# Expert weights in 2 MB transfers, gate and up by column halves, and a spare slot used once

## The reference, cut to what matters

```python
h = h + HybridMixer(RMSNorm(h)); h = h + MemXAttn(RMSNorm(h), mem); h = h + MoE(RMSNorm(h)); out = RMSNorm(h)

# MoE: top 4 of 32 experts for each token, w_gate, w_up, w_down: (32, 1024, 1024) float32
glu = xb @ w_gate[e] + b_gate[e]
lin = xb @ w_up[e] + b_up[e]
glu = minimum(glu, 7.0); lin = clip(lin, -7.0, 7.0)
y = (glu * sigmoid(1.702 * glu) * (lin + 1.0)) @ w_down[e] + b_down[e]
out[token] += gate[token, e] * y
```

## Time and profile before

| | us |
|---|---|
| median of 3 runs | 1294.68 (1294.14 to 1295.74) |
| the profiled execution | 1294.88 |
| its span | 1293.0 |
| PE busy in it | 1162.2 (90%) |
| DVE busy | 411.7 (32%) |
| ACT busy | 260.5 (20%) |
| DMA | 458.08 MB, mean 354 GB/s |

### The profile page before, as it was taken

How to read it: one execution, slowest core, us unless ns; L and a number is a source line. 1 busy time by engine, 2 the same in 40 slices (tenths; PEclk the granted TensorE clock), 3 DMA queues, 4 the chain that set the end, 5 groups by cost and what they waited for, 6 DMA issues and landing times.

```text
span 1293.0 us, 16762 instructions
## 1 busy us (share of the span) xinstructions
PE 1162.2 (90%) x6655; PEld 594.6 (46%) x6655; DVE 411.7 (32%) x819; ACT 260.5 (20%) x460; POOL 20.2 (2%) x43
## 2 busy tenths in 40 slices
PE   6999999998999999898889888988988899889886
PEld 5888888987433333343223333323333233233322
DVE  5689454566413221122122112111222221121112
ACT  5556354446311010010001001000110010001001
POOL 4000000000000000000000000000000000000000
PEclk9999999999999999999999999999999999999998
DMA  8565433697399999999999999999999999999993
GB/s 280 178 206 176 158 116 115 229 339 311 120 417 422 420 420 421 421 422 422 422 422 422 422 421 422 422 422 422 422 422 422 421 422 422 422 422 422 422 422 141
DMA packets 103988, 458.08 MB, mean 354 GB/s; under 512 B 7308, under 2 KB 50392, under 8 KB 54792
## 3 DMA queue, kind: packets, MB, share of 16 engines
q1 hardware_dynamic: 103008, 455.11, 87.6%
q0 software_dynamic: 848, 2.33, 0.6%
q10 hardware_dynamic: 88, 0.02, 0.0%
HBM read 456.39 MB, written 1.05 MB: 354 GB/s over the span
## 4 chain that ended last, share of the span: by engine, by line
PE 60%; DMA 28%; DVE 6%; ACT 3%; issue 2%; SPq 2%; DVEq 0%; POOL 0%; POOLq 0%; ACTq 0%
DMA ring<-in_w_up 27%; PE bank L1686 22%; PE bank L1713 11%; PE bank L1307 7%; PE bank L1330 5%; PE bank L1380 5%; PE bank L1644 2%; SPq L384 2%; PE bank L1442 1%; DVE ring L854 1%; PE bank L1654 1%; ACT reg_t L521 1%; PE bank L1699 1%; ACT ring L544 1%; DMA ring<-in_w_in 1%
## 5 line engine op out<-in xcount | busy, mean ns | idle before, releaser
L1686 PE MATMUL bank<-ring,reg_a 128*64 128x512 f32 x2048 | 457.7, 595 | 61.3 <-DMA ring<-in_w_up 60.7
L1686 PEld LDWEIGHTS bank<-ring,reg_a 128*64 128x64 f32 x2048 | 154.6, 137 | 351.6 <-issue 349.3
L1713 PE MATMUL bank<-ring,reg_g 128*64 128x512 f32 x1024 | 238.7, 621 | 21.4 <-DVE reg_g L1257 21.4
L1236 DVE COPY reg_t<-bank 128x512 f32<-128x512 f32 x32 | 22.1, 692 | 612.2 <-PE bank L1686 612.2
L521 ACT ACTIVATE reg_t<-bank 128x512 f32<-128x512 f32 x64 | 38.2, 597 | 679.2 <-PE bank L1686 472.6
L1713 PEld LDWEIGHTS bank<-ring,reg_g 128*64 128x64 f32 x1024 | 75.3, 142 | 178.4 <-issue 140.7
L854 DVE SCALAR_TENSOR_TENSOR ring<-ring 128x2048 f16<-128x2048 f32 x36 | 82.3, 2290 | 47.2 <-ACT ring L544 47.1
L544 ACT ACTIVATE ring<-ring 128x2048 f16<-128x2048 f32 x36 | 68.5, 1907 | 17.3 <-PE bank L1380 6.8
L1307 PE MATMUL bank<-reg_a,ring 128*128 128x256 f16 x576 | 66.6, 279 | 3.4 <-DVE reg_a L862 3.4
L1654 PE MATMUL bank<-reg_t,reg_g 64*128 64x512 f32 x256 | 63.6, 615 | 5.6 <-ACT reg_t L521 5.6
L1380 PE MATMUL bank<-reg_a,ring 128*128 128x256 f16 x576 | 63.2, 273 | 0.0
(11 more groups left out here) (252 smaller groups left out, 781.4 us busy)
## 6 DMA issues: line engine op xcount, KB each, us to landing
ring<-in_w_gate SPq DMA_DIRECT2D x128, 1024.0 KB, 26.5
ring<-in_w_up SPq DMA_DIRECT2D x128, 1024.0 KB, 27.0
ring<-in_w_down SPq DMA_DIRECT2D x128, 1024.0 KB, 26.9
ring<-in_w_in SPq DMA_DIRECT2D x24, 1024.0 KB, 5.4
ring<-in_w_branch_gate SPq DMA_DIRECT2D x8, 1024.0 KB, 5.4
ring<-in_w_xkv SPq DMA_DIRECT2D x4, 1024.0 KB, 5.2
ring<-in_w_mix_out SPq DMA_DIRECT2D x4, 1024.0 KB, 5.4
ring<-in_w_branch_gla SPq DMA_DIRECT2D x2, 1024.0 KB, 4.9
```

The costliest lines, as they stand in the source:

```text
L1686: ins = mm(pt[nh][col:col + 64, :], xe[c], w[:, i, nh * 512:(nh + 1) * 512], start=(c == 0), stop=(c == C - 1))
L1713: ins = mm(pt[2][64 * nh:64 * nh + 64, :], actT[:, c, :], w[:, i, nh * 512:(nh + 1) * 512], start=(c == 0), stop=(c == C - 1))
```

## The change

- A slot is 2 MB (128 partitions x 4096 floats, 16 KB each) and there are 8. A transfer is 2 MB, so an expert has 6 units: gate 0, up 0, gate 1, up 1, down 0, down 1.
- Gate and up lie in memory by column halves: unit 0 holds the first 512 columns for all 8 row chunks, unit 1 the others. PE finishes bank 0 first, then bank 1. Down stays by row chunks, four in a unit.
- The regions `reg_o` and `reg_l` are one, and its first 4096 floats are `spare`, a ninth slot in which unit 8 (gate 1 of the second expert) is loaded, once. `oxT` moves to `reg_t` and `gateT` behind the spare. POOL loads `b_down` and `final_norm_g`, whose places lie in the spare, after the second expert's gate and up.
- Between the dense halves five 2 MB units are issued, one for every second half; the spare and the units 5 to 7 follow.
- The units 9 and 10 are loaded in halves of 1 MB each, as PE has used the first and the last four row chunks of units 0 and 1.
- The second column half's transposes come after the scatter of the expert before.
- The last group is written out. Its last expert takes its weights as gate 0, up 0, down 0, gate 1, up 1, down 1, the last three in 2, 2 and 4 pieces, and computes in that order; the down biases are added ahead of it. `over` is computed by POOL during routing (ACT sums the excess), and the branch is ahead of the last group.
- At the end DVE multiplies by `gfin` while ACT squares, and scales in place afterwards.
- The rounds that are not run get semaphores of their own.

```diff
-NSLOT = 16
+NSLOT = 8
+WIDE = 2 * UNIT
...
-        slot = [region(ring, s * UNIT, UNIT) for s in range(NSLOT)]
+        slot = [region(ring, s * WIDE, WIDE) for s in range(NSLOT)]
...
-        oxT = parts(reg_o, 0, 4)
-        gateT = region(reg_o, 1024, T)
+        oxT = parts(reg_t, 0, 4)
+        gateT = region(reg_l, 2560, T)
+        spare = region(reg_ol, 0, WIDE)
...
-        def slot_of(v):
-            return (v + 2 * EARLY) % NSLOT
+        ORDER = [(0, 0), (1, 0), (0, 1), (1, 1), (2, 0), (2, 1)]
+        LAST_ORDER = [(0, 0), (1, 0), (2, 0), (0, 1), (1, 1), (2, 1)]
+        UPE = len(ORDER)
+        SPARE = NSLOT
+        FIRST_PIECES = {SPARE + 1: 2, SPARE + 2: 2}
+        LAST_PIECES = {UPE * EG - 3: 2, UPE * EG - 2: 2, UPE * EG - 1: 4}
+        piece_ld = {(v, i): sem(f"piece_ld{v}_{i}") for v, n in (*FIRST_PIECES.items(), *LAST_PIECES.items())
+                    for i in range(n - 1)}
+        spare_ld = sem("spare_ld")
+        def turn_of(v, z, first):
+            return v if z is more_rounds or (first and v < SPARE) else v - 1
+        def home_of(v, z, first):
+            if first and v == SPARE:
+                return spare, spare_ld, 0
+            w = turn_of(v, z, first)
+            s = (w + EARLY) % NSLOT
+            return slot[s], z.late_ld[s], 16 * (w // NSLOT + 1)
...
-            body(0, 0, True)
-            with eng.Fori(1, GROUPS) as n:
-                body(n, n, False)
+            body(0, 0, first_round, True, False)
+            with eng.Fori(1, GROUPS - 1) as n:
+                body(n, n, first_round, False, False)
...
+            body(GROUPS - 1, GROUPS - 1, first_round, False, True)
...
-            def load(v, e):
+            def load(v, e, z, first=False, order=ORDER, piece=0, count=1):
+                m, q = order[v % UPE]
+                home, done, _ = home_of(v, z, first)
+                n = WIDE // count
+                o = piece * n
+                src = mats[m][bass.ds(e, 1), :, q * WIDE + o:q * WIDE + o + n]
+                if piece < count - 1:
+                    done = piece_ld[v, piece]
+                sp.dma_start(home[:, o:o + n], src.rearrange("e p n -> p (e n)")).then_inc(done, 16)
+            def unit_left(v, e0, z):
                 m, q = ORDER[v % UPE]
-                s = slot_of(v)
-                src = mats[m][bass.ds(e, 1), :, q * UNIT:(q + 1) * UNIT]
-                sp.dma_start(slot[s], src.rearrange("e p n -> p (e n)")).then_inc(late_ld[s], 16)
-            def slot_left(v, e0):
-                m, q = ORDER[(v - NSLOT) % UPE]
-                e = (v - NSLOT) // UPE
-                if q < 3:
-                    sp.wait_ge(dn_used if m == 2 else gu_used, 3 * e0 + (3 * e + q + 1))
+                e = v // UPE
+                if m < 2:
+                    sp.wait_ge(z.h_full, 2 * e0 + (2 * e + q + 1))
                 else:
-                    sp.wait_ge(y_full if m == 2 else h_full, e0 + (e + 1))
+                    sp.wait_ge((z.dn_used, z.y_full)[q], e0 + (e + 1))
...
-                    load(v, v // UPE)
+                    elif i < EARLY:
+                        dense_left(2 * i)
+                        dense_left(2 * i + 1)
+                    load(v, v // UPE, first_round, True)
...
-                if u >= HALVES.index("mix0"):
+                if u >= HALVES.index("mix0") and (u - HALVES.index("mix0")) % 2 == 0:
                     first_units(1)
             per = UPE * EG
-            first_units(per - first[0])
-            def body(n, k):
+            take(sp, "xs3")
+            load(SPARE, SPARE // UPE, first_round, True)
+            first_units(NSLOT - first[0])
+            for piece in range(2):
+                for v in FIRST_PIECES:
+                    sp.wait_ge((first_round.gu_used, first_round.h_full)[piece], 1)
+                    load(v, v // UPE, first_round, True, ORDER, piece, 2)
+            for v in range(SPARE + 3, per):
+                before = v - NSLOT - 1
+                unit_left(before if before < SPARE else before + 1, 0, first_round)
+                load(v, v // UPE, first_round, True)
+            def body(n, k, z, last=False):
                 for v in range(per):
-                    slot_left(v, k * EG)
-                    load(v, n * EG + v // UPE)
-            with sp.Fori(1, GROUPS) as n:
-                body(n, n)
+                    unit_left(v - NSLOT, k * EG, z)
+                    if last and v >= per - UPE:
+                        count = LAST_PIECES.get(v, 1)
+                        for piece in range(count):
+                            load(v, n * EG + v // UPE, z, False, LAST_ORDER, piece, count)
+                    else:
+                        load(v, n * EG + v // UPE, z)
...
-            take(pool, "xo11")
+            root(6, 8)
+            emptied(pool, "all")
+            pool.tensor_scalar(over[:], st[:, 60:61], 0.0, None, ALU.is_gt).then_inc(over_ready, 1)
+            pool.wait_ge(first_round.h_full, 2 * (SPARE // UPE) + 2)
             pool.dma_start(b_dn[0:E, :], A["b_down"][0]).then_inc(ld_late, 16)
             pool.dma_start(gfin, A["final_norm_g"].rearrange("(a n) -> a n", a=1).to_broadcast([P, D]))\
                 .then_inc(ld_late, 16)
-            root(6, 8)
-            pool.wait_ge(ld_late, 16 * 2)
...
+            dve.wait_ge(ld_late, 16 * 2)
+            for t in range(TT):
+                dve.wait_ge(acc_full, 2 * t + 2)
+                gained(t, 1)
+                dve.wait_ge(fin_ss, 2 * t + 1)
+                gained(t, 0)
+                asked(t)
+            dve.wait_ge(fin_gain, 2 * TT)
+            for t in range(TT):
+                scaled(t)
...
+            def down_biases():
+                pe.wait_ge(ld_late, 16 * 2)
+                for t in range(TT):
+                    for n in range(2):
+                        mm(acc[t][n][:], gateT[0:E, t * P:(t + 1) * P], b_dn[0:E, n * 512:(n + 1) * 512],
+                           start=False, stop=False)
...
+                def gate_up(j, nh, v):
+                    for c in range(C):
+                        if j == 0 and nh == 0 and c % 2 == 0:
+                            pe.wait_ge((z.xg_act, z.xg_dve)[c // 2 % 2], 2 * k + (c // 4 + 1))
+                        for i, col in enumerate((0, 64)):
+                            ins = mm(pt[nh][col:col + 64, :], xg[:, c, j * SLOTS:(j + 1) * SLOTS],
+                                     loaded(v + i, C, c), start=(c == 0), stop=(c == C - 1))
+                        if nh == 0 and c == 3:
+                            ins.then_inc(z.gu_used, 1)
+                        if j == 0 and nh == 0 and c == 1:
+                            gather(2)
+                            gather(3)
+                    ins.then_inc(z.h_full, 1)
+                def hidden_T(j, i):
+                    pe.wait_ge((z.hs_act, z.hs_dve)[i], k * EG + (j + 1))
+                    for c in range(4):
+                        ins = pe.transpose(pt[i][:, c * P:(c + 1) * P], hs[:, 4 * i + c, :], ident[:])
+                    ins.then_inc(z.T_full, 1)
+                def down(j, i, v):
+                    pe.wait_ge(z.act_ready, k * 2 * EG + (2 * j + i + 1))
+                    for c in range(4):
+                        w = loaded(v, 4, c)
+                        for nh in range(2):
+                            ins = mm(pt[2][64 * nh:64 * nh + 64, :], actT[:, 4 * i + c, :],
+                                     w[:, nh * 512:(nh + 1) * 512], start=(i == 0 and c == 0), stop=(i == 1 and c == 3))
+                    ins.then_inc((z.dn_used, z.y_full)[i], 1)
...
+                    if last and j == EG - 1:
+                        down_biases()
+                        gate_up(j, 0, v)
+                        scatter(j - 1)
+                        hidden_T(j, 0)
+                        down(j, 0, v + 2)
+                        gate_up(j, 1, v + 3)
+                        hidden_T(j, 1)
+                        down(j, 1, v + 5)
+                        continue
+                    gate_up(j, 0, v)
+                    gate_up(j, 1, v + 2)
...
+                    for i in range(2):
+                        down(j, i, v + 4 + i)
...
-    for name in ("w_gate", "w_up", "w_down"):
+    for name in ("w_gate", "w_up"):
         w = np.asarray(inputs[name])[0]
-        inputs[name] = w.reshape(E, C, P, D).transpose(0, 2, 1, 3).reshape(E, P, C * D)
+        inputs[name] = w.reshape(E, C, P, 2, D // 2).transpose(0, 2, 3, 1, 4).reshape(E, P, C * D)
+    w = np.asarray(inputs["w_down"])[0]
+    inputs["w_down"] = w.reshape(E, C, P, D).transpose(0, 2, 1, 3).reshape(E, P, C * D)
```

276 lines of the change are left out of this document (139 added, 137 removed).

## The result

The changed kernel takes 1286.02 us (median of 4 runs, 1283.76 to 1286.76) against 1295.12 for the kernel before: the ratio is 0.9928 with a 95% interval of 0.9913 to 0.9944. That is 9.1 us faster, where the prediction's sum had 13.8. The profiled execution took 1286.76 us, the longest of the four, with a span of 1284.8.

A forecast was written before the change was run, and what follows sets the result against it. The DMA stream of expert weights was taken as the bound; -13.9 - 5.0 + 1.8 - 0.1 + 1.6 + 0.2 + 1.6 = -13.8 us gave 1281 us, range 1268 to 1295.

The forecast's parts named there:

- The bound: Expert stage: the DMA stream of weights sets the pace, 119.3 us per four experts with TensorE busy 104.0.
- The rate: Expert weight stream: 16 KB rows raise 422 to 428.6 GB/s, 0.077 us for each of 181 transfers, -13.9 us.
- Rival (1): Expert weight stream: no gain in rate from longer rows, so -13.9 us falls away: 1290 to 1298 us, chance 0.13.
- The first release: Start of the expert stream: the first half slots come free at 353.4 us, later than before, +1.8 us.
- The hole: Early expert stream: a 0.4 us gap as large as before, -0.1 us; later releases precede an empty queue, tightest by about 1 us.
- rival (3): Early stream or each group's start: releases in larger steps let the load queue run dry, 1285 to 1300 us, chance 0.05.
- The spare: Ahead of the experts: 18 MB instead of 16 are loaded, so 366 MB stay instead of 368, -5.0 us.
- the late loads: `b_down` and `final_norm_g`, 0.65 MB, leave the idle stretch and share the full stream after the second expert's gate/up, +1.6 us.
- The branch: Overflow test and its branch, one group earlier: beside a full queue they cost 0.
- The end: After the flow's last byte: 23.8 us by the TensorE walk plus 2 for clock falls, against 24.2 before, +1.6 us.
- Rival (2): TensorE in the expert groups: its clock falls at the new waits and it becomes the bound, 1313 us, chance 0.05.

The follow-up runs named there:

- `pp_no_spare`: `pp_branch` without the spare slot: 1278.64 us (ratio 0.9879 to the kernel before).
- `no_spare`: The changed kernel without the spare slot, `b_down` and `final_norm_g` loaded in the idle stretch again: 1285.92 us (ratio 0.9927 to the kernel before).
- `pp_branch`: `last_plain` with gate 1 and up 1 of the last expert in halves, down biases in the first group, overflow branch after the fifth: 1276.03 us (ratio 0.9855).
- `last_plain`: The changed kernel with its last expert loaded and computed in the order of all others (gate, up, then down): 1278.23 us (ratio 0.9867).
- `halves_15_16`: The changed kernel with units 15 and 16 also loaded in halves of 1 MB, the first halves issued earlier: 1285.67 us (ratio 0.992).

## Why the prediction was right in its direction, and 5 us too low

- **The bound**: right. The DMA sets the pace from 401 us on, at 428 GB/s through every group up to the last.
- **The rate, -13.9**: right in mechanism, 2 us too much in size. The steady stretches are at 428, where 428.6 was taken, which over 181 transfers is 1.2 us by this estimate; with rows of 8 KB put back the time rises by 11.5 to 11.8, as a slower drain also feels less of the early stream's holes. Rival (1) is out.
- **The first release, +1.8**: right (352.85 against 353.4; the first expert also began 0.76 us earlier than before, at 347.15).
- **The hole, -0.1, "by about 1 us"**: this is the step that failed. The walk's own times, flow from 353.4 + 1.45 on and a hole of 0.4 us, mean 400 GB/s between 352 and 401 us. The trace has 376, which is 24 x 49 / 428 = 2.7 us of flow less. With the 1.2 us of the rate that gives, as an estimate, the 3.9 us by which the flow ended late (1257.3 against 1253.4), and the last expert's data came late by about as much. The walk used 7.09 us for the first down matmuls, which stand behind an idle 2.35 us, although the prediction itself showed such a stretch with 8.78. It is rival (3) in a small way: the late releases, not a dry steady state.
- **The spare, -5.0, with the late loads, +1.6**: too much by 0.8 us. Where the end waits for data the two are worth 2.6 (`pp_no_spare`) and not 3.4, since the early stretch moves less with the spare. In the changed kernel the medians with and without it are equal, but the two traces differ by a start of the last expert 2.2 us later and by two falls of the clock (`no_spare`), so nothing else was measured there.
- **The branch, 0, "beside a full queue"**: the reason was incomplete. The queue was full, but TensorE pays 5.26 us (2.62 before), waits for no load from there on, and reaches the last expert 1.2 us behind the data. The size stands as far as it was tested: `pp_branch` takes out this branch and the biases, TensorE then waits 4.5 us for the data, and the median doesn't move (1276.03 against 1275.82). The end waits for the later of two, and both were late.
- **The end, +1.6**: its steps were right (gate/up 7.09, scatter 1.99, wait ahead of the down 2.42, then 7.03), its clock falls were two of 1.6 us (3.25 in all where 2 us were taken), and the steps behind the last copy took some 0.8 more than 9.1. What it left out was the comparison. It walked the new order and set 25.8 us behind the flow beside the old 24.2, but never walked the old order with the new transfers. That would have shown that loading the last half late is paid for with a second chain of transposes and activations on TensorE: `last_plain` needs 34.6 us from the start of the last expert's gate/up where the changed kernel needs 43.8, and takes 7.8 us less in all.
- **Rival (2)**, the clock: falls do come (the granted clock is 0.96 in the steady stretch, 0.99 before), but TensorE's busy time for four experts rose only from 103.95 to 109.38 us, and the rate held. Its price was met where TensorE's own way sets the time: at the first down, at the last wait for data (`halves_15_16`, `last_plain`) and in the last expert. In the changed kernel the gate/up matmuls behind a wait of 2.70 us took 8.78 us (from 1101.82) and those behind 2.67 took 7.08 (from 1131.19). The Trainium skill's rule ("TensorE: Matmul & The Clock Gate", HAM oscillation), a fall at each wait for data, is thus half of what the trace shows: falls come at some of the waits, and where the DMA is the bound they cost nothing.

What stays open: the holes at 352 to 401 differ between executions of nearly the same program, with and without a fall of the clock, and no kernel here fixes that clock alone, so the fall's share in the late data is bounded (at most the 2.9 us by which `pp_branch`, whose first down matmuls kept their clock, moved more in that stretch: 25 x 49 / 428) and not measured. Nor is it known why the same wait is followed by a fall in one execution and not in another.
